# One weight unit loaded ahead of another expert's, a final gain row spread by TensorE, router products before two transposes

## The chip, the cores and the metric

The kernel runs on one core of a Trainium2 chip. The time is the device time of one execution in microseconds (us), and the times of the kernel before are a median of three runs. The engines are named as in the profile: PE is TensorE, DVE is VectorE, ACT is ScalarE, POOL is GpSimd and SP is SyncE. SPq and POOLq are the queues from which SP and POOL issue DMAs. PE is in order: what is written first is done first.

## The reference

A decoder trunk of two layers on 256 tokens of 1024 channels in float32. Each layer adds a mixer, a cross-attention into 256 memory tokens and a feed-forward part; the first layer's is dense, the second's picks two of eight experts for each token. A last norm follows.

```python
def moe_swiglu(xn, router_w, w13, w2):
    logits = (xt @ router_w).astype(jnp.float32)
    top_vals, top_idx = lax.top_k(logits, TOP_K)              # TOP_K = 2, N_EXPERTS = 8
    top_p = jax.nn.softmax(top_vals, axis=-1)
    ...
    for e in range(N_EXPERTS):
        out = out + gates[:, e:e + 1] * swiglu(xt, w13[e], w2[e])   # w13[e]: 1024 x 7168, w2[e]: 3584 x 1024
...
x = x + moe_swiglu(hn, router_w[layer // 2], w13_moe[layer // 2], w2_moe[layer // 2])
return rmsnorm(x, final_norm_g)
```

## The kernel before

**Experts as items.** The eight experts are eight "items". Item 0 and the even ones have room for 96 tokens ("mid", `mid_x`), item 1 and the odd ones for 64 ("few", `few_x`). The weights of an item are 42 units of 1 MiB (`ITEM_UNITS`), read in seven steps j = 0..6: four units of the up projection, then two of the down projection of the step before. So 336 units pass through the chip, each is loaded once and used once, in float32. The order in which PE reads them is the list `READS`: 12 units of item 0 (`HEAD`, two steps), the whole of item 1, the other 30 of item 0 (`BODY`), then items 2 to 7. Item 0's expert is fixed, so its units may be loaded before the router has decided; item 1's may not.

**Buffers and the order of loads.** There are 20 slots of 1 MiB (`RING`), and a twenty-first (`slot_once`, `pool_at`) that is used once. The list `LOADS` is the order in which SP issues the loads: 20 units of item 0 (`EARLY`), the 42 of item 1, the other 22 of item 0, then items 2 to 7. Below, load n is the entry n of that list, counted from 0. `rooms_of_loads()` gives each load after the twentieth the slot of a unit already read, and SP waits on `units_read` until PE has read it: load 20 waits for the first read, and from load 35 on load n waits for read n-19. One load, `EXTRA`, goes into `slot_once` and waits on `routed`, which DVE raises at the end of the routing. SP issues strictly in order. Between the 20 early loads and load 20 it waits on `info_ready` (L573) and reads two values (`info`: the number of items, item 1's expert).

**Steps of one item on PE.** In `item()`, PE calls `between(j)`, then transposes `hidden` (L2316), multiplies four up units (L2252) and two down units (L2252). ACT applies Silu (L987) and copies the transposed hidden values (L978); DVE multiplies (L1644). `between(j)` is where other work is put into an item: `lay_out`, `back`, `gather_pair`, and in the last item `lay_x` (L2214), four products of 128x512 that lay the residual stream into PSUM.

**Router.** The residual stream `x` is transposed on PE (`turn_plain` L1805, `turn_quarter` L2103) and `route()` (L2113) forms the logits from the transposed halves. The last quarter of `x` comes from DVE in two parts (`x_quarter`, `x_part`, L1387). ACT and DVE copy the transposes out (`lower_xT`, `quarter_xT`, `upper_xT`). From the logits DVE finds the two experts of each token, the places and the order of the items.

**Gains.** The weights of each norm are one row of 1024 values. `load_gain` on POOL (L614) reads the row 128 times over, 512 KB, into `g_row` on 128 partitions, as soon as the norm before has used the old one. The last norm's go this way too. DVE uses them first in item 7 (`weigh_x`) and ACT and DVE write the output after that.

## Time and profile before

| what | value |
|---|---|
| median of 3 runs (lowest, highest) | 1334.89 us (1334.65, 1335.25) |
| the profiled execution, its own time | 1334.52 us |
| its span, first to last instruction | 1332.7 us |
| granted clock of TensorE, mean | 0.998 |
| PE busy | 1310.0 us (98%) |
| DVE, ACT, POOL busy | 407.1, 333.3, 14.8 us |
| DMA moved | 444.27 MB |
| expert weights among it | 336 units of 1024 KB |

The page gives busy times of each engine and cuts the span into 40 equal slices (33.3 us each) with a digit for the share of each. The slices of the expert part begin with the sixteenth, at about 500 us. In them both PE and DMA show digits of 9, so the page alone does not say which of the two limits the expert part; that has to be read from the waits and from the time that a load takes from its issue to its landing. A matmul of float32 is two records in the trace (x8 are four), and successive records overlap, so a price is read from the distance of their starts.

### The profile page before, as it was taken

Reading aid. Unit: us, or ns where it says so; the run is one execution under the profiler, and the core shown is the slowest. Engines: PE = TensorE matmul, PEld = TensorE weight load, DVE = VectorE, ACT = ScalarE, POOL = GpSimd, SP = SyncE. Lnnn points to the kernel's source line nnn. Section 1 sums busy time; section 2 is a strip of 40 time slices with the busy share of each in tenths; the row PEclk is TensorE's granted clock in tenths of the full one; section 3 lists DMA queues with packets and bytes.
Section 4 is the critical chain, followed back from the end, with each engine's and each line's share of the span. In section 5 each row is a group of like instructions: output and inputs, shape, how many; then the busy total and the mean of one; then the engine's idle time right before and its main releaser. Section 6 shows DMA issues by size and latency. Waiting matters only on the chain.

```text
span 1332.7 us, 24929 instructions
## 1 busy us (share of the span) xinstructions
PE 1310.0 (98%) x10817; PEld 857.7 (64%) x10817; DVE 407.1 (31%) x778; ACT 333.3 (25%) x629; POOL 14.8 (1%) x28
## 2 busy tenths in 40 slices
PE   9999999999999999998999999999999999999987
PEld 6989888888798986432667666335666335666322
DVE  6686754444748765000111100101100101100201
ACT  6565554443646642000001000001000001000002
POOL 1100000000000000000000000000000000000000
PEclk9999999999999999999999999999999999999999
DMA  8935255554543689999999999999999999999995
GB/s 322 336 130 225 95 188 186 187 187 187 185 178 120 250 341 368 405 423 421 420 420 420 420 408 396 413 420 420 420 420 419 420 421 420 419 421 419 421 421 241
DMA packets 63913, 444.27 MB, mean 333 GB/s; under 512 B 7293, under 2 KB 8717, under 8 KB 10936
## 3 DMA queue, kind: packets, MB, share of 16 engines
q1 hardware_dynamic: 61976, 437.22, 81.4%
q0 software_dynamic: 1824, 5.42, 1.1%
q8 instruction: 87, 1.43, 0.4%
q14 instruction: 26, 0.21, 0.0%
HBM read 441.17 MB, written 1.44 MB: 332 GB/s over the span
## 4 chain that ended last, share of the span: by engine, by line
PE 91%; DMA 4%; SPq 2%; DVE 2%; ACT 1%; issue 1%; DVEq 0%; ACTq 0%
PE up_banks L2252 34%; PE bank L2252 16%; PE bank L1752 7%; PE bank L1754 7%; PE bank L1753 7%; DMA raw<-in_moe_units 4%; PE up_banks L1752 3%; PE up_banks L1754 3%; PE up_banks L1753 3%; SPq L536 2%; PE bank L2316 1%; PE bank L2199 1%; PE bank L1847 1%; PE bank L2229 1%; PE bank L1794 1%; DVE w_lo L1053 1%
## 5 line engine op out<-in xcount | busy, mean ns | idle before, releaser
L1644 DVE TENSOR_TENSOR hidden<-hidden,up_banks 128x384 f32<-128x384 f32 (+1 forms) x56 | 27.3, 487 | 582.7 <-ACT hidden L987 582.7
L1053 DVE TENSOR_TENSOR w_lo<-raw,w_hi 128x1024 fp32r<-128x1024 f32 x154 | 181.5, 1219 | 42.0 <-ACT w_hi L660 40.7
L660 ACT ACTIVATE w_hi<-raw 128x1024 fp32r<-128x1024 f32 x154 | 155.2, 1057 | 47.6 <-PE bank L1754 39.6
L987 ACT ACTIVATE hidden<-up_banks 128x384 f32<-128x384 f32 (+1 forms) x56 | 24.5, 437 | 475.3 <-PE up_banks L2252 475.3
L2252 PE MATMUL up_banks<-raw,mid_x 128*32 128x256 f32 (+1 forms) x1260 | 95.0, 450 | 0.0
L2252 PE MATMUL bank<-raw,hT 128*32 128x256 f32 (+2 forms) x716 | 82.1, 486 | 2.7 <-DMA raw<-in_moe_units 2.6
L1752 PE MATMUL bank<-xT_hi,w_hi 128*128 128x256 f32 x288 | 82.5, 287 | 0.0
L1753 PE MATMUL bank<-xT_lo,w_hi 128*128 128x256 f32 x288 | 81.5, 283 | 0.0
L1754 PE MATMUL bank<-xT_hi,w_lo 128*128 128x256 f32 x288 | 81.4, 283 | 0.0
L2252 PEld LDWEIGHTS up_banks<-raw,mid_x 128*32 128x32 f32 x1260 | 57.4, 110 | 33.3 <-issue 1.6
L978 ACT ACTIVATE hT<-bank 128x384 f32<-128x384 f32 (+1 forms) x56 | 24.5, 437 | 209.2 <-PE bank L2316 209.2
L2252 PE MATMUL up_banks<-raw,few_x 128*64 128x512 f32 x296 | 67.7, 595 | 0.5 <-DMA raw<-in_moe_units 0.5
L2252 PEld LDWEIGHTS bank<-raw,hT 128*32 128x32 f32 (+1 forms) x716 | 38.7, 116 | 41.2 <-issue 25.1
L1752 PEld LDWEIGHTS bank<-xT_hi,w_hi 128*128 128x128 f32 x288 | 55.2, 192 | 1.4 <-issue 1.3
L1753 PEld LDWEIGHTS bank<-xT_lo,w_hi 128*128 128x128 f32 x288 | 55.2, 192 | 0.1
L1754 PEld LDWEIGHTS bank<-xT_hi,w_lo 128*128 128x128 f32 x288 | 55.2, 192 | 0.0
L1752 PE MATMUL bank<-w_hi,yT_hi 128*128 128x512 f32 x136 | 53.7, 395 | 0.4 <-DVE w_lo L1053 0.3
L1754 PE MATMUL bank<-w_hi,yT_lo 128*128 128x512 f32 x136 | 53.0, 390 | 0.0
L1753 PE MATMUL bank<-w_lo,yT_hi 128*128 128x512 f32 x136 | 52.9, 389 | 0.0
L2252 PE MATMUL up_banks<-slot_w_hi,mid_x 128*32 128x256 f32 (+1 forms) x648 | 50.3, 451 | 0.0
L2252 PE MATMUL up_banks<-slot_w_lo,mid_x 128*32 128x256 f32 (+1 forms) x612 | 47.5, 450 | 0.0
L2252 PEld LDWEIGHTS up_banks<-raw,few_x 128*64 128x64 f32 x296 | 20.6, 137 | 40.5 <-issue 39.1
(421 smaller groups left out, 2099.7 us busy)
## 6 DMA issues: line engine op xcount, KB each, us to landing
raw<-in_moe_units SPq DMA_DIRECT2D x109, 1024.0 KB, 23.0
slot_w_hi<-in_moe_units SPq DMA_DIRECT2D x46, 1024.0 KB, 23.8
slot_w_lo<-in_moe_units SPq DMA_DIRECT2D x46, 1024.0 KB, 24.2
raw<-in_layer_units SPq DMA_DIRECT2D x44, 1024.0 KB, 4.9
raw<-in_dense_units SPq DMA_DIRECT2D x33, 1024.0 KB, 4.8
slot_bias<-in_moe_units SPq DMA_DIRECT2D x19, 1024.0 KB, 22.7
slot_xT_lo<-in_moe_units SPq DMA_DIRECT2D x18, 1024.0 KB, 22.9
slot_xT_hi<-in_moe_units SPq DMA_DIRECT2D x18, 1024.0 KB, 22.8
```

Source lines behind the costliest of these rows:

```text
L536: sp.dma_start(slots[slot], src).then_inc(sem(f"in{slot}"), 16)
L660: act.activation(w_hi[:, st.split(u), half, :], raw[:, st.slot(u), half * n:(half + 1) * n], ACT.Copy)\
L978: act.activation(hT[:, j % 2, 0:n, :], bank[3][:, 0:n * P].rearrange("p (b r) -> p b r", b=n), ACT.Copy)\
L987: act.activation(hidden_of(n), ups_of(n, 1), ACT.Silu).then_inc(sem("silu"), 1)
L1053: dve.tensor_tensor(w_lo[:, st.split(u), half, :], raw[:, st.slot(u), half * n:(half + 1) * n], w_hi[:, st.split(u), half, :].bitcast(F32) ...
L1644: dve.tensor_tensor(hidden_of(n), hidden_of(n), ups_of(n, 0), ALU.mult)\
L1752: pe.matmul(out, hi_l, hi_r, start=start, stop=False, skip_group_check=True)
L1753: pe.matmul(out, hi_l, lo_r, start=False, stop=False, skip_group_check=True)
L1754: return pe.matmul(out, lo_l, hi_r, start=False, stop=stop, skip_group_check=True)
L1794: mm = pe.transpose(bank[b][:, k * P:(k + 1) * P], xn[:, t, a:a + P], ident)
L1847: pe.matmul(bank[6][:, :], conv_u[:, 0, 0:P], conv_u[:, :, 0:T], start=True, stop=True)
L2252: return pe.matmul(out, rows, moving, start=start, stop=stop, skip_group_check=True)
```

## The change

Three things are changed.

1. `AHEAD = RING + 1`: one more unit of item 0 (the twenty-first of `HEAD + BODY`) is loaded before item 1's units, and SP issues it before it waits on `info_ready`. It waits for the first read. `EXTRA`, the load into `slot_once`, becomes item 1's unit 1 in place of its unit 2, so that it is still load 22. Every unit of item 1 is one place later in `LOADS`; from load 63 on the order is as before.
2. The last norm's gains are loaded as one row of 4 KB (POOL, same wait) and spread to 128 partitions by two PE products of 128x512 (`spread_gain`) with a row of ones, in item 2 ahead of step 5; ACT copies them out in two (`gain_rows`), before that step's Silu. DVE waits for those copies (`last_gain`) in item 7 in place of the DMA.
3. `route(0, 0)`, four products, stands before the two `turn_quarter`s instead of between them.

```diff
--- before.py
+++ after.py
@@ -60,6 +60,7 @@
 HEAD = (*range(10), 14, 15)
 BODY = tuple(u for u in range(ITEM_UNITS) if u not in HEAD)
 EARLY = (HEAD + BODY)[:RING]
+AHEAD = RING + 1
 
 
 SKEW_W, SKEW_P = 384, 32
@@ -239,11 +240,11 @@
 
 LATER = [unit for i in range(2, NE) for unit in whole(i)]
 READS = of_first(HEAD) + whole(1) + of_first(BODY) + LATER
-LOADS = of_first(EARLY) + whole(1) + of_first((HEAD + BODY)[RING:]) + LATER
+LOADS = of_first((HEAD + BODY)[:AHEAD]) + whole(1) + of_first((HEAD + BODY)[AHEAD:]) + LATER
 
 
 READ_NO = {unit: n + 1 for n, unit in enumerate(READS)}
-EXTRA = (1, 2)
+EXTRA = (1, 1)
 
 
 def rooms_of_loads():
@@ -489,6 +490,7 @@
     last_banks = (6, 7, 1, 5)
     weighed_bank = 0
     pair_banks = (2, 6, 7)
+    gain_banks = (2, 6)
     xlogit_banks = (2, 3, 6, 7)
 
     def heads_of_pair(b, t):
@@ -569,6 +571,13 @@
         for n in range(1, RING):
             hold(sp, *room[n])
             load_unit(item_units(0), EARLY[n], moe[EARLY[n]])
+
+        def load_first(units):
+            for u in units:
+                hold(sp, "units_read", item_units(0).room(u))
+                load_unit(item_units(0), u, moe[u])
+
+        load_first((HEAD + BODY)[RING:AHEAD])
         sp.wait_ge(sem("info_ready"), 1)
         n_items = sp.value_load(info[0:1, 0:1], min_val=NE, max_val=ITEMS)
 
@@ -582,9 +591,7 @@
                 load_unit(item_units(i), u, moe[e * ITEM_UNITS + u])
 
         load_item(1)
-        for u in (HEAD + BODY)[RING:]:
-            hold(sp, "units_read", item_units(0).room(u))
-            load_unit(item_units(0), u, moe[u])
+        load_first((HEAD + BODY)[AHEAD:])
         for i in range(2, NE):
             load_item(i)
         with sp.If(n_items > NE):
@@ -643,7 +650,10 @@
                 pool.dma_start(less8[:, :, :], io["less8"]).then_inc(sem("router_in"), 16)
                 pool.dma_start(row_ids[:, :], io["row_ids"]).then_inc(sem("router_in"), 16)
             load_gain(l * 3 + 3, io["ffn_norm_g"][l])
-            load_gain(l * 3 + 4, io["mix_norm_g"][l + 1] if l + 1 < DEPTH else io["final_norm_g"])
+            if l + 1 < DEPTH:
+                load_gain(l * 3 + 4, io["mix_norm_g"][l + 1])
+        pool.wait_ge(sem("xn_ready"), (3 * DEPTH + 1) * 4)
+        pool.dma_start(g_row[0:1, :], io["final_norm_g"].rearrange("(o d) -> o d", o=1)).then_inc(sem("gain_in"), 16)
 
 
     @block.scalar
@@ -970,6 +980,12 @@
                 last = act.activation(to[:, 512:768], bank[5][:, 0:256], ACT.Copy)
             last.then_inc(sem("y_hi"), 1)
 
+        def gain_rows():
+
+            act.wait_ge(sem("gain_mm"), 1)
+            for half, b in enumerate(gain_banks):
+                act.activation(g_row[:, half * 512:(half + 1) * 512], bank[b][:, :], ACT.Copy).then_inc(sem("last_gain"), 1)
+
         def item(i, units, many, begin=0, end=ITEM_STEPS, first_in=None):
             n = 3 if many else 2
 
@@ -983,6 +999,8 @@
                     if j == 1 and first_in is not None:
                         first_in()
                     turned_hidden(j - 1)
+                if j == 5 and isinstance(i, int) and i == 2:
+                    gain_rows()
                 act.wait_ge(sem("units_read"), units.read(3 if j == 0 else 6 * j + 1))
                 act.activation(hidden_of(n), ups_of(n, 1), ACT.Silu).then_inc(sem("silu"), 1)
             turned_hidden(end - 1)
@@ -1689,7 +1707,7 @@
                                              iota[:, 0:FEW].unsqueeze(1).broadcast_to([P, 2, FEW]), 1.0,
                                              pos[:, t, i:i + 1], ALU.add, ALU.is_equal)
                 last.then_inc(sem("select"), 1)
-                dve.wait_ge(sem("gain_in"), 16 * (3 * DEPTH + 1))
+                dve.wait_ge(sem("last_gain"), 2)
                 dve.wait_ge(sem("added"), i * 4)
                 weigh_x()
             gated(i, 3, many)
@@ -2115,9 +2133,9 @@
             if upper:
                 mm.then_inc(sem("router_mm"), 1)
 
+        route(0, 0)
         pe.wait_ge(sem("x_quarter"), 1)
         turn_quarter(4, 7).then_inc(sem("quarter_mm"), 1)
-        route(0, 0)
         pe.wait_ge(sem("x_part"), 4 * (3 * DEPTH - 2) + 4)
         turn_quarter(6, 1).then_inc(sem("xT_mm"), 1)
         route(0, 1)
@@ -2218,6 +2236,13 @@
 
             pe.wait_ge(sem("weighed_x"), times)
             pe.matmul(bank[weighed_bank][:, :], ident, weighed_x[:, :], start=True, stop=False, skip_group_check=True)
+
+        def spread_gain():
+
+            pe.wait_ge(sem("gain_in"), 16 * (3 * DEPTH + 1))
+            for half, b in enumerate(gain_banks):
+                mm = pe.matmul(bank[b][:, :], mats[0:1, 2, :], g_row[0:1, half * 512:(half + 1) * 512], start=True, stop=True)
+            mm.then_inc(sem("gain_mm"), 1)
 
         def lay_out(i):
 
@@ -2389,6 +2414,8 @@
                 elif j == 3:
                     pe.wait_ge(sem("added"), i * 4)
                     lay_out(i)
+                elif j == 5 and i == 2:
+                    spread_gain()
                 elif j == 4 and i == NE - 1:
                     weigh_rows(i)
                 elif j == 6 and i == NE - 1:
```

On SP, at the end of the early loads. Before (the names are the slots; `slot_bias_49` is the slot of the very first unit):

```order
L536 DMA slot_yT_lo_62<-in_moe_units 128x2048 [waits unit_used]
L573 TENSOR_LOAD info [waits info_ready]
L573 ISA x2
L576 TENSOR_LOAD info
L576 ISA x2
L536 ISA [waits units_read]
L536 DMA slot_bias_49<-in_moe_units 128x2048
L536 ISA [waits units_read]
L536 DMA raw<-in_moe_units 128x2048
L536 ISA [waits routed]
L536 DMA slot_once<-in_moe_units 128x2048
```

After the change:

```order
L538 DMA slot_yT_lo_62<-in_moe_units 128x2048 [waits unit_used]
L538 DMA slot_bias_49<-in_moe_units 128x2048 [waits units_read]
L582 TENSOR_LOAD info [waits info_ready]
L582 ISA x2
L585 TENSOR_LOAD info
L585 ISA x2
L538 ISA [waits units_read]
L538 DMA raw<-in_moe_units 128x2048
L538 ISA [waits routed]
L538 DMA slot_once<-in_moe_units 128x2048
L538 ISA [waits units_read]
L538 DMA raw<-in_moe_units 128x2048
```

The load into `slot_bias_49` has moved from behind the wait on `info_ready` and the two value loads to ahead of them.

On PE, the end of the last projection and the router products (`mats,x` are transposes of x, `plain_xT,pool_inv` the router products). Before:

```order
L1805 MATMUL bank<-mats,x 128x128 [waits x_part,router_gain]
L1805 MATMUL bank<-mats,x 128x128 x3
L2103 MATMUL bank<-mats,x 128x128 [waits x_quarter]
L2103 MATMUL bank<-mats,x 128x128
L2113 MATMUL up_banks<-plain_xT,pool_inv 32x128 [waits lower_xT]
L2113 MATMUL up_banks<-plain_xT,pool_inv 32x128 x3
L2103 MATMUL up_banks<-mats,x 128x128 [waits x_part]
L2103 MATMUL up_banks<-mats,x 128x128
L2113 MATMUL up_banks<-plain_xT,pool_inv 32x128 [waits upper_xT]
L2113 MATMUL up_banks<-plain_xT,pool_inv 32x128 x3
L2113 MATMUL bank<-plain_xT,pool_inv 32x128 [waits lower_xT]
```

After the change:

```order
L1823 MATMUL bank<-mats,x 128x128 [waits x_part,router_gain]
L1823 MATMUL bank<-mats,x 128x128 x3
L2131 MATMUL up_banks<-plain_xT,pool_inv 32x128 [waits lower_xT]
L2131 MATMUL up_banks<-plain_xT,pool_inv 32x128 x3
L2121 MATMUL bank<-mats,x 128x128 [waits x_quarter]
L2121 MATMUL bank<-mats,x 128x128
L2121 MATMUL up_banks<-mats,x 128x128 [waits x_part]
L2121 MATMUL up_banks<-mats,x 128x128
L2131 MATMUL up_banks<-plain_xT,pool_inv 32x128 [waits upper_xT]
L2131 MATMUL up_banks<-plain_xT,pool_inv 32x128 x3
L2131 MATMUL bank<-plain_xT,pool_inv 32x128 [waits lower_xT]
```

The router products with `lower_xT` have moved above both transposes, so the second transpose follows the first directly.

On PE in item 2, between the second down unit of step 3 and step 5's first up unit. Before:

```order
L2252 MATMUL bank<-raw,hT 32x512 [waits in2]
L2252 MATMUL bank<-raw,hT 32x512 x2
L2252 MATMUL bank<-raw,hT 32x256 x6
L2252 MATMUL bank<-raw,hT 32x512 x3
L2252 MATMUL bank<-raw,hT 32x256 x6
L2316 MATMUL bank<-mats,hidden 128x128 [waits hid_ready]
L2316 MATMUL bank<-mats,hidden 128x128 x2
L2252 MATMUL up_banks<-raw,mid_x 32x512 [waits in3]
L2252 MATMUL up_banks<-raw,mid_x 32x512 x2
L2252 MATMUL up_banks<-raw,mid_x 32x256 x6
L2252 MATMUL up_banks<-raw,mid_x 32x512 x3
```

After the change:

```order
L2277 MATMUL bank<-slot_xT_hi_51,hT 32x512 x2
L2277 MATMUL bank<-slot_xT_hi_51,hT 32x256 x6
L2277 MATMUL bank<-slot_xT_hi_51,hT 32x512 x3
L2277 MATMUL bank<-slot_xT_hi_51,hT 32x256 x6
L2244 MATMUL bank<-g_row,mats 128x512 [waits gain_in]
L2244 MATMUL bank<-g_row,mats 128x512
L2341 MATMUL bank<-mats,hidden 128x128 [waits hid_ready]
L2341 MATMUL bank<-mats,hidden 128x128 x2
L2277 MATMUL up_banks<-slot_w_hi_52,mid_x 32x512 [waits in7]
L2277 MATMUL up_banks<-slot_w_hi_52,mid_x 32x512 x2
L2277 MATMUL up_banks<-slot_w_hi_52,mid_x 32x256 x6
```

Two rows of 128x512 with `g_row` stand ahead of the transposes of `hidden` that were there before.

## Rows read from the trace of the kernel before

**Rows 1.** The page: its span, its GB/s by 40 slices, one DMA issue line.
```profile
span 1332.7 us, 24929 instructions
...
GB/s 322 336 130 225 95 188 186 187 187 187 185 178 120 250 341 368 405 423 421 420 420 420 420 408 396 413 420 420 420 420 419 420 421 420 419 421 419 421 421 241
...
g_row<-in_final_norm_g POOLq DMA_DIRECT2D x1, 512.0 KB, 9.9
```

**Rows 2.** Windows: stretch and length, busy PE PEld DVE ACT POOL, PEclk, DMA, GB/s.
```profile
515.00:520.00 5.00, 5.00 (x76) 3.13 (x72) 4.55 (x23) 0.61 (x1) 0.00 (x0) 1.00 0.71 282
520.00:525.00 5.00, 5.00 (x61) 2.78 (x54) 0.53 (x2) 0.49 (x1) 0.00 (x0) 1.00 0.89 356
...
631.00:718.00 87.00, 86.95 (x1134) 57.18 (x1136) 8.92 (x20) 7.27 (x17) 0.00 (x0) 1.00 1.01 420
718.00:770.00 52.00, 52.00 (x694) 34.99 (x690) 7.55 (x15) 3.81 (x8) 0.00 (x0) 1.00 1.01 420
770.00:840.00 70.00, 70.00 (x903) 43.30 (x896) 3.24 (x6) 4.79 (x10) 0.00 (x0) 1.00 1.00 398
```

**Rows 3.** Chain of waits, end of item 1 and end of the span: start, length, what.
```profile
603.74 25.30 DMA raw<-in_moe_units
...
1293.99 26.35 DMA raw<-in_moe_units
1320.39 1.96 PE bank L2252 x8
```

**Rows 4.** Timeline of SP's issues: start, length, what.
```profile
518.04 0.36 SPq L536 DMA_DIRECT2D slot_bias<-in_moe_units  x1
518.99 0.34 SPq L536 DMA_DIRECT2D raw<-in_moe_units  x1
...
534.40 0.33 SPq L536 DMA_DIRECT2D slot_xT_hi<-in_moe_units  x1
```

**Rows 5.** Timeline of PE in item 0's head: the units' first records.
```profile
515.95 7.96 PE L2252 MATMUL up_banks<-raw,mid_x 128*32 128x512 f32 x108
...
531.37 2.79 PE L2252 MATMUL up_banks<-slot_xT_hi,mid_x 128*32 128x512 f32 x36
533.95 2.80 PE L2252 MATMUL up_banks<-slot_w_hi,mid_x 128*32 128x512 f32 x36
```

**Rows 6.** Line L536, 457:469: four lone loads, issue to landing.
```profile
L536 SPq DMA_DIRECT2D raw<-in_moe_units x4: 327/328/328, 457.9 to 468.0; - x4
...
DMA to landing us min/median/max: 4.6/4.9/5.0
```

**Rows 7.** The same of load 20 alone, issued at 518.04.
```profile
L536 SPq DMA_DIRECT2D slot_bias<-in_moe_units x1: 360/360/360, 518.0 to 518.0; - x1
...
DMA to landing us min/median/max: 5.1/5.1/5.1
```

**Rows 8.** The same of load 32 alone, issued at 548.40.
```profile
L536 SPq DMA_DIRECT2D slot_memT_lo<-in_moe_units x1: 333/333/333, 548.4 to 548.4; - x1
...
DMA to landing us min/median/max: 6.6/6.6/6.6
```

**Rows 9.** The same of load 145 alone, late in item 2.
```profile
L536 SPq DMA_DIRECT2D slot_w_lo<-in_moe_units x1: 333/333/333, 834.9 to 834.9; - x1
...
DMA to landing us min/median/max: 6.9/6.9/6.9
```

**Rows 10.** Timeline of PE at the router: last transposes and the router products.
```profile
502.71 0.60 PE L1805 MATMUL bank<-mats,x 128*128 128x128 f32 x4
503.39 0.44 PE L2103 MATMUL bank<-mats,x 128*128 128x128 f32 x2
503.76 0.43 PE L2113 MATMUL up_banks<-plain_xT,pool_inv 128*32 128x128 f32 x8
504.11 0.44 PE L2103 MATMUL up_banks<-mats,x 128*128 128x128 f32 x2
504.48 0.43 PE L2113 MATMUL up_banks<-plain_xT,pool_inv 128*32 128x128 f32 x8
```

**Rows 11.** Timeline of PE in item 7: products of 128x512 in float32 (`lay_x`).
```profile
1304.28 1.02 PE L2214 MATMUL up_banks<-x,mats 128*128 128x512 f32 x2
1305.14 1.02 PE L2214 MATMUL bank<-x,mats 128*128 128x512 f32 x2
1305.99 0.38 PE L2316 MATMUL bank<-mats,hidden 128*128 128x128 f32 x2
```

## The prediction

> **What bounds the kernel now.** The page's GB/s line comes first [rows 1]: from the expert part on it stands at about 420, whatever PE does. 1024 KB at 420 GB/s is 2.49 us for one unit. The chain of waits says where that matters. Item 1 ends with a load issued at 603.74 that lands 25.30 us later, and the span ends with one issued at 1293.99 that lands 26.35 us later, after which PE has only its last unit left [rows 3]. With lone loads landing in 4.6 to 5.0 us [rows 6], the other 20 us of each are queue: the DMA stream is the limit, and the end moves with the place of the last load in it. From the last landing to the end nothing is changed that takes time.
>
> Two places can move that stream. The first is its gap. In 515:520 the DMA share is 0.71 and in 520:525 it is 0.89 [rows 2], some 2.0 us without data, because load 20 is issued only at 518.04 [rows 4]. The second is where the queue is nearly empty, since there a later issue costs time at once. In a mid item PE takes 2.58 us for a unit (starts at 531.37 and 533.95 [rows 5]), plus its turns, against the stream's 2.49, so through items 0 and 2 PE loses ground and the slots come free later and later. The loads' times to landing tell how much is left: 6.6 us for load 32 [rows 8] and 6.9 us for load 145 at 834.9 [rows 9]. If a lone load takes 4.9 us, the median of [rows 6], load 32 has 1.7 us of queue before it and load 145 has 2.0 us. After that item 3, a few item, refills the queue. Between 631 and 840 PE is busy 208.95 of 209 us [rows 2], so what is added to PE there is added to every read behind it.
>
> **Router products ahead of the turns.** PE's second quarter turn starts at 504.11, and between it and the first stand four products (eight records) that start at 503.76 [rows 10]. In front of both turns they fall partly into the gap between the last half's transposes, about 0.44 us of issue from 502.71, and the first turn at 503.39. The first turn then starts some 0.12 us later; the second, on which the last copies and products hang, starts at about 503.88 in place of 504.11. I take 0.23 us, between nothing (if a copy of ACT ends last) and 0.36, the distance of such a group's starts. All of the routing, PE's first expert unit and all later issues by reads move by it.
>
> **One more load ahead.** An issue follows PE's next unit by 0.45 us: the unit at 533.95 [rows 5] and the issue at 534.40 [rows 4]. The first read is marked by the unit at 515.95 [rows 5], so the new load 20 goes out at 516.40, less 0.23, 516.17, in place of 518.04. It is alone, so it lands after 4.9 to 5.1 us [rows 6, 7]. Load 21 is set by the second read already (518.99 [rows 4], 518.76 with the 0.23) and lands at 523.7, against 518.04 + 5.1 + 2.49 = 525.6 before. So the stream gains 1.9 to 2.0 us there. Later issues follow reads as before, and at load 32 the gain can be no more than its queue and the 0.23: 1.7 + 0.23 = 1.9 us. Both bounds agree; I take 1.9. If lone loads take 4.6 us it is 2.0, with 5.1 it is 1.7.
>
> This is not yet the end. Item 1's units have moved one place back, and PE reads its last one as it lands [rows 3]. That landing shifts by 2.49 - 1.9 = +0.6 us. PE begins the rest of item 0 0.6 us later, and has no idle time in which to make it good.
>
> **The gain row.** The DMA of 512 KB becomes 4 KB. At 420 GB/s that is 1.2 us of transfer; it was issued at about 506.5 and took 9.9 us to land [rows 1], so all of it lies ahead of the gap. The early loads land 1.2 us sooner, PE doesn't read them yet, and the gap only starts sooner: worth nothing. In exchange PE gets two products of 128x512. The nearest rows are those of item 7, whose starts stand 0.86 us apart (1304.28, 1305.14, and the next work at 1305.99) [rows 11]: 1.72 us, all added since PE is never idle there. The bounds are 0.9 us, if the single row makes them cheaper, and 2.0 us with a bubble at the change of shape. ACT's two copies lie in its wait for the up products, on its own queue ahead of one Silu whose units last 10 us; they cost nothing. DVE's new wait, in item 7, was met long before. SP has one issue moved, none added.
>
> **The sum.** In item 2 PE is late by 0.6 + 1.72 = 2.3 us, and load 145's issue with it. It has 2.0 us of queue before it, and what isn't covered shifts its landing: +0.3 us. From there the stream runs without a gap to the end, so the end moves by +0.3 us, and the 1.9 us gained at 518 are gone: between the two places PE's reads, not the stream, hand on the time. With L for a lone load, the shift is 2.49 - (6.6 - L + 0.23) + 1.72 - (6.9 - L) = 2L - 9.5 us: -0.3 for 4.6, +0.3 for 4.9, +0.7 for 5.1. The profiled execution took 1334.52 us, its span 1332.7; the sum gives 1334.8. The median of the runs stands 0.37 us above it, so I predict 1334.89 + 0.3 = **1335.2 us**.
>
> The Trainium skill, page "DMA: Bandwidth & Descriptors", section "Anatomy of one DMA", fits a DMA as 2.0 us plus bytes over 436 GB/s. That is 4.4 us for a unit, and an estimate by it gives -0.7 us. Its fit is for POOL's path; rows 6 have 4.6 to 5.0 and decide.
>
> **Rivals.**
>
> *The stream keeps its gain.* If PE's lateness never reaches an empty queue, the end moves by the 1.9 us gained in the gap: 1333.0 us. That takes no more than 0.1 us of lateness in item 2 at L = 4.9, or units that take longer than PE's 2.58, so that the queue grows in mid items too. The GB/s of 398 in 770:840 against 420 [rows 2] speaks a little for it: the stream itself is slow there. Against it speaks 6.9 us at load 145, the end of a queue that has been shrinking. Chance 0.15. The same page's "Specifications" gives a limit of about 358 GB/s per core, by which a unit would take 2.93 us and this rival would hold; rows 2 with 420 say otherwise, and the chance stands as it was.
>
> *The load ahead is not early.* If it lands no sooner than the old load 20 did, because PE's first read comes about when the values are read, only the 0.23 is left of the gain: 2.49 - 0.23 + 1.72 - 2.0 = +2.0 us, 1336.9 us. It decides by the issue of load 20: at 516.2 it is wrong, near 518 right. The read at 515.95 speaks against it. Chance 0.10. This one is slower than before, as is the next.
>
> *A load behind another needs more than a lone one.* The term 2L takes both queues as usable down to the last 4.9 us. If a load with one other in flight can't land in under 6.1 us, the shift is 2 x 6.1 - 9.5 = +2.7 us, and from there on the change is slower by over 0.2%; at 6.5 us it is +3.5 us, 1338.4 us. The trace shows 6.6 as the least in the expert stream outside the gap, which leaves it open; load 20's 5.1 is against it. Chance 0.07.
>
> **How the numbers follow.** The forecast, with L from 4.6 to 5.1 and the products from 0.9 to 2.0 us, gets 0.65; 0.03 is left for what I don't see. Its own range is 1334.0 to 1336.0. The range of 8 in 10 takes in the first two rivals: **1333.0 to 1336.9 us**. What a measurement of this kernel can tell from no change is 0.2%, 2.7 us. Slower by more than that is the third rival, 0.07; faster by more than that needs over 2.7 us where the gap has 2.0, 0.03; within it 0.90.
>
> **What would show it.** Load 20 issued near 516.2 and landing in about 5 us. Item 1's last unit landing 0.6 us later than at 629.0. PE's two products 1.7 us together in item 2. Load 145 issued about 2.3 us later and landing in about 4.9 us instead of 6.9: that is the step that decides. If it still takes 6 us or more, the sum is wrong in PE's terms; if load 32 does not fall towards 4.9, it is wrong in the gap's. The last landing would be at about 1320.6. If the pauses that the stream makes by itself (398 GB/s) come elsewhere, all of this shifts by some tenths.

## The result: 4.2 us slower, and the profile after

The changed kernel takes 1339.05 us, median of 9 runs (1337.23 to 1340.22), against 1334.89 us for 9 runs of the kernel before (1332.9 to 1336.28). The ratio is 1.0032, interval [1.0024, 1.0040]: slower by 3.2 to 5.3 us. The forecast was 1335.2 us and its range ended at 1336.9.

The profiled execution of the changed kernel took 1340.22 us, the slowest of its nine runs, so its trace may hold something that a median run doesn't. The page of after, to be read beside [rows 1] (span, GB/s in 40 slices):

```profile
span 1338.4 us, 24939 instructions
...
GB/s 319 344 131 214 102 195 186 188 187 189 184 157 147 247 332 378 391 422 422 420 420 420 409 406 355 408 421 421 420 419 420 421 421 420 419 420 419 421 421 226
```

In the expert part the difference is in the slices (33 us each) just behind the gap (17th: 391 instead of 405 GB/s) and in those of item 2 (23rd to 26th: 409, 406, 355, 408 instead of 420, 408, 396, 413). From the 27th on both kernels move 420 GB/s. The chain of waits (start, length, what) says the same at its two landings, the end of item 1 and the end of the span:

```profile
605.71 25.13 DMA slot_w_lo<-in_moe_units
...
630.89 1.94 PE bank L2277 x8
...
1298.69 26.36 DMA raw<-in_moe_units
...
1325.09 1.96 PE bank L2277 x8
```

Item 1's last unit lands at 605.71 + 25.13 = 630.84, and before at 603.74 + 25.30 = 629.04 [rows 3]: it is 1.8 us later. PE begins the last unit of all at 1325.09 instead of 1320.39 [rows 3], 4.7 us later. The work of PE, ACT and DVE behind that is as long as before (DVE's last instruction starts at 1333.55 instead of 1328.85, 4.7 us later too). The output's DMA behind it ends 1.0 us later still; from the last landing to the end the traces take 12.4 to 13.7 us, whatever the kernel, and the kernel before has the least of it. So the traces are compared below by this landing and not by their spans.

**The head** (the first units of item 0, around the gap at 518). SP's issues (timeline: start, length, what), to be read beside [rows 4]:

```profile
515.64 0.33 SPq L538 DMA_DIRECT2D slot_bias<-in_moe_units  x1
518.38 0.36 SPq L538 DMA_DIRECT2D raw<-in_moe_units  x1
519.66 0.34 SPq L538 DMA_DIRECT2D slot_once<-in_moe_units  x1
```

Load 20 is issued at 515.64 (forecast 516.17, before 518.04) and lands 5.0 us later, as forecast. Yet the windows (columns as in [rows 2]) show that the stream does not stay full behind it:

```profile
515.00:520.00 5.00, 5.00 (x76) 3.14 (x72) 3.98 (x19) 0.00 (x0) 0.00 (x0) 1.00 0.74 275
520.00:525.00 5.00, 5.00 (x57) 2.40 (x49) 0.95 (x3) 0.49 (x1) 0.00 (x0) 1.00 0.91 321
...
770.00:840.00 70.00, 70.00 (x912) 43.76 (x904) 2.22 (x4) 4.91 (x10) 0.00 (x0) 0.98 0.95 380
```

The rest of the gap only moves: 275 GB/s instead of 282 in the first 5 us, 321 instead of 356 in the next. By the trace's landings load 20 is in 2.6 us earlier than before and load 21 2.3 us earlier, but load 33 only 0.2 us. In 770:840, where load 145 stands, the stream moves 380 GB/s instead of 398 [rows 2].

**Load 145.** The line of SP's loads, at the issue of load 145 (first line: durations in ns and start), and what it took to land:

```profile
L538 SPq DMA_DIRECT2D slot_memT_lo<-in_moe_units x1: 333/333/333, 840.3 to 840.3; - x1
...
DMA to landing us min/median/max: 7.0/7.0/7.0
```

It is issued 5.4 us later than before (840.3 against 834.9 [rows 9]) and still takes 7.0 us where it took 6.9. The forecast had it fall to 4.9. So at load 145 nothing of PE's 5.4 us of lateness is absorbed in this execution. Yet loads a little before it did come down to the time of a lone one, those issued at 808.0 (load 133) and at 824.1 to 829.3 (loads 139 to 141), each while the load before it was still in flight:

```profile
L538 SPq DMA_DIRECT2D slot_w_lo<-in_moe_units x1: 333/333/333, 808.0 to 808.0; - x1
...
DMA to landing us min/median/max: 4.9/4.9/4.9
...
DMA to landing us min/median/max: 5.1/5.2/5.3
```

Loads 142 and 145 then land 3.8 and 4.0 us after the one before instead of 2.49, and that brings load 145 back to 7.0. So the queue was used up, and the stream lost time on top of that.

**PE in item 2** (timeline: start, length, what):

```profile
795.52 2.82 PE L2277 MATMUL bank<-slot_xT_hi,hT 128*32 128x512 f32 x36
798.27 1.98 PE L2244 MATMUL bank<-g_row,mats 1*128 1x512 f32 x4
800.18 0.55 PE L2341 MATMUL bank<-mats,hidden 128*128 128x128 f32 x3
800.66 4.49 PE L2277 MATMUL up_banks<-slot_w_hi,mid_x 128*32 128x512 f32 x36
804.95 2.78 PE L2277 MATMUL up_banks<-slot_w_lo,mid_x 128*32 128x512 f32 x36
```

The two products of `spread_gain` (line 2244) hold PE from 798.27 to the start of the next work at 800.18: 1.9 us, forecast 1.72. The unit behind them takes 4.49 us where its neighbours take 2.8, and the granted clock says why (windows, the same columns, PEclk third from the end):

```profile
802.00:803.00 1.00, 1.00 (x12) 0.45 (x8) 0.00 (x0) 0.23 (x1) 0.00 (x0) 0.50 0.99 418
803.00:804.00 1.00, 1.00 (x10) 0.54 (x6) 0.00 (x0) 0.00 (x0) 0.00 (x0) 0.50 0.58 229
804.00:805.00 1.00, 1.00 (x17) 0.52 (x13) 0.00 (x0) 0.00 (x0) 0.00 (x0) 0.60 0.12 49
805.00:806.00 1.00, 1.00 (x18) 0.59 (x14) 0.00 (x0) 0.00 (x0) 0.00 (x0) 1.00 0.00 0
```

For some 3.4 us TensorE ran at half clock (0.5, which is 1.2 of 2.4 GHz), though PE was never idle ahead of it. That costs 1.7 us, and the DMA share falls to 0 behind it: the queue was empty. The Trainium skill, page "TensorE: Matmul & The Clock Gate", section "What's actually happening", has these two levels and ties the lower one to an engine that was not busy. The trace doesn't agree: here PE had been busy without a break, with two products whose operands hold 1 of 128 rows just ahead.

So there were two candidates for the 4.2 us. **Theory A**: the clock. The products of one row make it fall, and that is most of the loss. **Theory Q**: the queue, which is the prediction's third rival. A load behind others needs more time than a lone one, so neither the gain in the gap nor load 145's 2.0 us is really there, and each microsecond of PE goes to the end. The expectations of the first four runs name a **theory B** in its place, that the unit moved ahead of item 1 is what costs; **theory L**, in later ones, is the forecast's, by which the queue can be used down to 4.9 us.

### The profile page after: what moved, and what is told of

Read it like the earlier page. It is cut to its first block, busy times and chain, and to the rows that moved or that the text cites. A ratio compares the mean times of both kernels' runs of the same rounds, so it can differ in the third digit from the quotient of the medians.

```text
span 1338.4 us, 24939 instructions
## 1 busy us (share of the span) xinstructions
PE 1313.6 (98%) x10821; PEld 858.4 (64%) x10821; DVE 407.1 (30%) x778; ACT 334.8 (25%) x631; POOL 14.8 (1%) x28
## 4 chain that ended last, share of the span: by engine, by line
PE 77%; SPq 14%; DMA 5%; DVE 2%; issue 1%; ACT 1%; DVEq 0%; ACTq 0%
PE up_banks L2277 26%; SPq L538 14%; PE bank L2277 12%; PE bank L1770 7%; PE bank L1772 7%; PE bank L1771 7%; DMA slot_w_lo<-in_moe_units 3%; PE up_banks L1770 3%; PE up_banks L1772 3%; PE up_banks L1771 3%; DMA raw<-in_moe_units 2%; PE bank L2341 1%; PE bank L1865 1%; PE bank L1812 1%; PE bank L2217 1%
```

## The experiments

Each was timed in 5 rounds beside the kernel before, whose medians in the three groups that ran together were 1335.08, 1334.73 and 1334.68 us. Ratios are to it, with their 95% interval, and a time in brackets behind one is ratio minus 1 times 1335; its interval reaches some 1.2 us to either side. "PE at 145" is the shift against before, in the profiled execution, of the unit on which load 145's issue waits, and "last landing" that of the last load.

### The load ahead alone

```diff
+AHEAD = RING + 1
-LOADS = of_first(EARLY) + whole(1) + of_first((HEAD + BODY)[RING:]) + LATER
+LOADS = of_first((HEAD + BODY)[:AHEAD]) + whole(1) + of_first((HEAD + BODY)[AHEAD:]) + LATER
-EXTRA = (1, 2)
+EXTRA = (1, 1)
...
+        load_first((HEAD + BODY)[RING:AHEAD])
         sp.wait_ge(sem("info_ready"), 1)
```

> Before with part 1 alone (one more load of item 0 ahead, EXTRA moved). Theory A, PE's clock: the loss comes mainly from the one-row products, so here PE is late by 1.2 to 1.8 us at the end of item 1 (2.49 us less what the stream gains in its gap) and nothing is added in item 2; load 145's queue of 2 us covers it, and the end moves by -0.5 to +0.5 us. Theory B, the order of loads: the unit moved ahead of item 1 is what costs, and the end moves by +2 to +4 us. Load 20 should be issued at about 516.4 and no clock fall should appear in item 2 under either.

Measured: 1337.18 us, 1.0019 [1.0010, 1.0029] (+2.5 us). Its gap is closed better than in the changed kernel's trace, and the gain is lost all the same (windows):

```profile
515.00:520.00 5.00, 5.00 (x76) 3.11 (x68) 3.94 (x19) 0.00 (x0) 0.00 (x0) 1.00 1.01 393
520.00:525.00 5.00, 5.00 (x57) 2.40 (x48) 0.95 (x3) 0.49 (x1) 0.00 (x0) 1.00 0.99 398
530.00:555.00 25.00, 24.51 (x271) 13.16 (x260) 0.58 (x2) 1.91 (x4) 0.00 (x0) 1.00 0.96 371
```

In 530:555, some ten loads behind the gap, it moves 371 GB/s; the kernel before moved there:

```profile
530.00:555.00 25.00, 25.00 (x281) 13.58 (x270) 0.55 (x1) 1.52 (x3) 0.00 (x0) 1.00 1.01 408
```

37 GB/s for 25 us is 0.9 MB, 2.2 us of stream. Load 33 lands only 0.3 us earlier than before, item 1's last landing comes 2.4 us later, nearly the whole 2.49 us of the place, and both PE at 145 (+2.4) and the last landing (+2.5) follow. This part alone makes more than half of the loss: theory A's -0.5 to +0.5 us did not come, with no half clock at work.

### The gain row alone

```diff
+        pool.dma_start(g_row[0:1, :], io["final_norm_g"].rearrange("(o d) -> o d", o=1)).then_inc(sem("gain_in"), 16)
...
+                mm = pe.matmul(bank[b][:, :], mats[0:1, 2, :], g_row[0:1, half * 512:(half + 1) * 512], start=True, stop=True)
...
+                elif j == 5 and i == 2:
+                    spread_gain()
```

> Before with part 2 alone (gain row of 4 KB, two one-row products in item 2). Theory A: the granted clock falls to about 0.5 for 3 to 4 us right after the products, PE is late by 3.4 to 3.8 us from there on, load 145's queue of 2.0 us covers a part, and the end moves by +1.2 to +2.0 us. Theory B: the products cost 1.8 us, which the queue covers, and the end moves by 0 to +0.3 us.

Measured: 1337.00 us, 1.0012 [1.0003, 1.0021] (+1.6 us). PE at 145 is 1.95 us later, the two products, and the clock did not fall in its trace. The time lies in the range that was expected of theory A, but PE was not late by the 3.4 to 3.8 us that should have made it, so the number is no support for A. With the load ahead (+2.5) this makes 4.1 us, about the changed kernel's +4.2: within the intervals the parts add up, and no half clock is needed in the sum.

### Full rows in place of one row

On the changed kernel; it loads the 512 KB again and multiplies 128 rows by the identity.

```diff
-                mm = pe.matmul(bank[b][:, :], mats[0:1, 2, :], g_row[0:1, half * 512:(half + 1) * 512], start=True, stop=True)
+                mm = pe.matmul(bank[b][:, :], ident, g_row[:, half * 512:(half + 1) * 512], start=True, stop=True)
```

> The changed kernel, but the gains are loaded on all 128 partitions as before and the two products take all 128 rows of them against the identity matrix; same place, same size, same copies. Theory A (few rows at work let the clock fall): the clock stays at 1.00 in item 2, PE is late by 1.8 us less than in the changed kernel (3.6 in place of 5.4 us), and the end is 1.5 to 1.8 us earlier than the changed kernel's, some +2.9 us against before. If any change of shape of the products were enough for the clock, it falls here too and the end stays at +4 to +4.5 us.

Measured: 1339.70 us, 1.0033 [1.0020, 1.0045] (+4.4 us). There is no half clock in its trace, and it is no faster than the changed kernel. What A expected did not come. Nor did the 512 KB, which it loads again, cost anything that these medians can show.

### The products in item 1

On the changed kernel; they stand in step 5 of item 1, where PE waits for the stream.

```diff
+            elif j == 5:
+                pe.wait_ge(sem("spread"), 1)
+                spread_gain()
...
-                elif j == 5 and i == 2:
-                    spread_gain()
```

> The changed kernel with the two one-row products and their copies in item 1 ahead of step 5, where PE waits for loads anyway. Theory A: the clock may fall there too, but PE has about 0.8 us of idle time per unit there, so that item 1 still ends with its last landing; nothing is added in item 2 and the end moves by -0.5 to +0.8 us against before, that is 3.5 to 4.5 us less than the changed kernel. Theory B: the end stays at +2 to +4 us.

Measured: 1337.24 us, 1.0014 [1.0005, 1.0023] (+1.9 us). PE at 145 is +1.9 us, as it already is at the end of item 1: the products have vanished in PE's wait there. It is as fast as the load ahead alone. So what the products cost depends on their place.

### Two full products more, and four, in item 2

On the kernel before; their results are not used. The lines of the second have `range(4)`.

```diff
+        def more_products():
+
+            for n in range(2):
+                pe.matmul(bank[(2, 6)[n % 2]][:, :], ident, x[:, 0, 0:512], start=True, stop=True, skip_group_check=True)
...
+                elif j == 5 and i == 2:
+                    more_products()
```

> Before with two more full products of 128x512 on PE in item 2 ahead of step 5, into banks that nothing reads; nothing else is changed. PE is late by 1.72 us from there. Theory Q (a thin queue slows the stream long before it is empty; only latencies above about 7 us are free): hardly any of the lateness is covered at load 145 with its 6.9 us, and the end moves by +1.2 to +1.8 us. Theory L of the forecast (the queue can be used down to 4.9 us): the 2.0 us of queue cover it and the end moves by 0 to +0.3 us.

Measured: 1336.71 us, 1.0015 [1.0006, 1.0024] (+2.0 us).

> Before with four more full products of 128x512 on PE in item 2 ahead of step 5 (two in e5_two_more). PE is late by 3.4 us. Theory Q: nothing of it is covered beyond some tenths, the end moves by +3.0 to +3.6 us. Theory L: 2.0 us are covered, +1.4 us.

Measured: 1338.50 us, 1.0033 [1.0022, 1.0043] (+4.4 us). These two are nothing but PE time, at full rows, with no change to any load. The chain of waits of the one with two products, the end of item 1 and the end of the span:

```profile
603.47 25.31 DMA raw<-in_moe_units
...
628.82 1.94 PE bank L2257 x8
...
1296.04 26.31 DMA raw<-in_moe_units
...
1322.39 1.96 PE bank L2257 x8
```

Item 1's last unit lands 0.3 us earlier than before, and the last unit begins 2.0 us later [rows 3], with PE 1.5 us later at load 145. That load is issued at 836.4 and takes 8.1 us. By the prediction its 2.0 us of queue would have swallowed those 1.5.

### PE made earlier in item 2

On the kernel before. Four (the first) or two (the second) of item 2's accumulated blocks are left out, so that PE is 5.2 or 2.6 us faster there.

```diff
+                        if isinstance(i, int) and i == 2 and j in (2, 3) and k in (1, 3):
+                            continue
```

> Before with four of item 2's 56 row-block products of the up projection left out (channel blocks 1 and 3 in steps 2 and 3), so part of the expert's sum is missing; PE is 5.2 us earlier from about 770 on, the loads are the same. Theory Q: the queue at load 145 is deep enough to keep the pace, the extra pauses of loads 119 to 146 (3.8 us in the trace of before) largely go, and the end moves by -1 to -2.5 us. Rival (the pauses belong to the memory and come in any case, the stream is the limit throughout): the end does not move, within 0.3 us.

Measured: 1332.85 us, 0.9983 [0.9974, 0.9992] (-2.3 us).

> Before with two of the blocks of item 2 left out (channel blocks 1 and 3 of step 2, half of e10_item2_lighter), so part of that expert's sum is missing; PE is 2.6 us earlier. Theory Q: load 145 takes about 8.5 us, the stream keeps most of its pace, the end moves by -1.0 to -1.9 us, nearly all that e10 gave. If the rate rises only with a much deeper queue, it is half of e10's, -0.8 to -1.0 us.

Measured: 1333.26 us, 0.9992 [0.9983, 1.0001] (-1.1 us, which alone can't be told from none). The windows of 770:840, first with 5.2 us less:

```profile
770.00:840.00 70.00, 70.00 (x853) 41.95 (x845) 5.21 (x11) 5.08 (x11) 0.00 (x0) 1.00 1.01 420
```

and with 2.6 us less:

```profile
770.00:840.00 70.00, 70.00 (x875) 42.98 (x866) 4.66 (x9) 5.30 (x12) 0.00 (x0) 1.00 1.01 413
```

So the 398 GB/s of the kernel before [rows 2] were not a habit of the stream: with loads issued earlier it moves 420. In the lighter one load 145 took:

```profile
L536 SPq DMA_DIRECT2D slot_w_lo<-in_moe_units x1: 332/332/332, 828.9 to 828.9; - x1
...
DMA to landing us min/median/max: 11.8/11.8/11.8
```

In their traces PE is 3.6 us early at load 145 with two blocks less and 6.0 us with four, but the last landing only 2.4 and 1.7 us. The medians stand the other way round (-1.1 and -2.3 us), with intervals that overlap; both views say that earlier issues bring some 1 to 2.5 us and no more, though PE is early by up to 6. The kernel before thus already lost about 2 us in item 2 to a queue that was too short, at a load time of 6.9 us.

### The load ahead, with a lighter head

The load ahead alone, with two blocks of item 0's step 1 left out: PE is 2.6 us faster there.

```diff
+                        if isinstance(i, int) and i == 0 and begin == 0 and j == 1 and k in (1, 3):
+                            continue
```

> Part 1 alone (as in e1_ahead_only), with two of the products' blocks of item 0's step 1 left out, so part of that expert's sum is missing; the reads from the fifth on come up to 2.6 us sooner, and so the issues of loads 25 to 34. Theory Q: in e1 the gain of the gap was lost at loads 22 to 34 because the queue there was thin (6.5 to 7 us); here load 33 lands 1.5 to 2.5 us earlier than before, item 1's last read is late by +0.3 to +1.0 us in place of +2.4, and the end moves by 0 to +0.8 us against before in place of +2.5. Rival (the gain was lost to pauses of the memory's own): load 33 about -0.3 us, item 1 +2.4 us, as in e1.

Measured: 1334.38 us, 0.9995 [0.9986, 1.0004] (-0.7 us, within what can be told from none). Its window:

```profile
530.00:555.00 25.00, 24.06 (x254) 12.45 (x247) 0.98 (x2) 2.29 (x5) 0.00 (x0) 1.00 1.01 421
```

421 GB/s instead of 371. Load 21 lands 1.8 us earlier than before and load 33 still 1.6 us, and item 1's last unit 1.0 us earlier, where it was expected 0.3 us or more later. With its loads issued earlier the stream doesn't give the gain back in these ten loads, as it does with the load ahead alone. The kernel before with the same lighter head was not run, so how much of the 1.6 us at load 33 would be there without the load ahead is not shown.

### The changed kernel again

> The changed kernel once more, on this chip and beside these runs. If the fall of the granted clock behind the one-row products comes only in some executions, this profile may show none; then PE is late by 3.6 us in place of 5.4 us from step 5 of item 2 on and the time stays at +3.3 to +4.3 us against before. If the clock falls each time, it is there again at about 801 and lasts 3.4 us.

Measured: 1339.06 us, 1.0031 [1.0020, 1.0042] (+4.1 us), the same as the first time. In this profiled execution the clock stayed up (PE's timeline):

```profile
798.73 1.98 PE L2244 MATMUL bank<-g_row,mats 1*128 1x512 f32 x4
800.64 0.55 PE L2341 MATMUL bank<-mats,hidden 128*128 128x128 f32 x3
801.12 2.80 PE L2277 MATMUL up_banks<-slot_w_hi,mid_x 128*32 128x512 f32 x36
```

The unit behind the products takes 2.80 us, not 4.49, PE at 145 is +4.2 us instead of +5.4, and the last landing +3.9 instead of +4.7. So the half clock is an event of some executions, and is not the 4.2 us.

The mean granted clock that each run lists says how often. Half clock for 3.4 us takes 0.0013 off the mean over 1338 us. The mean is 0.998 or 0.999 in all 80 runs of the edited kernels that have no products of one row and in the 87 of the kernel before beside them. It is 0.997 in 12 of the 49 runs of the four kernels that have them: 5 of 16 of the changed kernel, 4 of 11 of the gain row alone, 3 of 11 of the last kernel below, 0 of 11 with the products in item 1 (a reading of 0.998 can hide a fall). So the fall belongs to the products of one row. The changed kernel's 5 runs at 0.997 have a mean of 1339.8 us, its 11 others 1338.7, which is still 3.8 us above the kernel before. The clock costs some 1.1 us where it falls, and theory A's main claim, that it is most of the loss, is wrong.

### The load ahead with the router products, and the rest without the load ahead

The changed kernel without part 2, and the kernel before with part 3 and the gain row in item 1, but without the load ahead.

```diff
+        route(0, 0)
         pe.wait_ge(sem("x_quarter"), 1)
         turn_quarter(4, 7).then_inc(sem("quarter_mm"), 1)
-        route(0, 0)
```

> The changed kernel without its part 2: one more load ahead and the router products ahead of the turns, the gains loaded as before. Theory Q: like part 1 alone, less the 0.2 to 0.3 us of the router: the end at +1.7 to +2.3 us against before, item 1's last read at +1.8 to +2.4 us, no lateness added in item 2.

Measured: 1337.10 us, 1.0019 [1.0010, 1.0028] (+2.5 us), no less than the load ahead alone, though in its trace item 1's last unit comes 1.3 us later than before and not 2.4. The router's 0.24 us is too little for these medians to show.

> Before with the router products ahead of the turns and the gain row of 4 KB, its two products in item 1 ahead of step 5, where PE waits for loads; no load is moved ahead. Theory Q: PE is not late in items 0 and 2, the 1.8 us of the products lie in its waits of item 1, and the end moves by -0.5 to 0.0 us. If the products or the clock cost something there, it is +0.5 us or more.

Measured: 1334.77 us, 1.0002 [0.9993, 1.0011] (+0.3 us). Without the load ahead and with the products under item 1's wait the change costs nothing, and brings nothing that can be told. No version here that computes the whole result beats the kernel before.

## Why the prediction was wrong, step by step

**One table shows it.** The shifts against the kernel before, in the profiled executions. "Pauses" is worked out from the landings: the sum, over loads 119 to 146, of what each lands later than 2.48 us after the one before it.

| kernel | PE at 145 | last landing | GB/s in 770:840 | pauses |
|---|---|---|---|---|
| item 2 lighter by 5.2 | -6.0 | -1.7 | 420 | 1.6 |
| item 2 lighter by 2.6 | -3.6 | -2.4 | 413 | 1.2 |
| router, gain row in item 1 | -1.6 | -1.9 | 404 | 1.9 |
| load ahead, lighter head | -1.0 | -1.5 | 396 | 4.1 |
| before | 0 | 0 | 398 | 3.7 |
| load ahead and router | +1.3 | +1.9 | 392 | 5.6 |
| two products more | +1.5 | +2.0 | 394 | 5.5 |
| changed, products in item 1 | +1.9 | +2.1 | 394 | 5.0 |
| gain row alone | +2.0 | +3.0 | 392 | 5.9 |
| load ahead alone | +2.4 | +2.5 | 392 | 5.8 |
| changed, full rows | +3.6 | +3.8 | 391 | 6.3 |
| changed, again | +4.2 | +3.9 | 387 | 7.3 |
| four products more | +4.3 | +3.5 | 387 | 5.6 |
| changed, with the half clock | +5.4 | +4.7 | 380 | 8.4 |

From about -2 us upward the end follows PE nearly one for one, whatever made PE late or early: a load, products of one row or of 128, or work left out. Below that it stops following. The prediction had put that bend at +2.0. The edits that change nothing but PE's work in item 2 (two lighter, two heavier) move the pauses too, so these don't come by themselves: the later the loads are issued, the more the stream pauses. Single executions scatter by one to two microseconds (the kernel before: 1332.9 to 1336.28), which the column of the last landing shows too.

**What the stream does.** From the issue and landing times of loads 22 to 335 in the fourteen traces one can work out how much longer than 2.48 us after the load before it each load lands, sorted by how long after its own issue the load before it lands. Where that is over 10 us, the mean excess is 0.02 to 0.05 us; from 5 us on it is at most 0.09; from 4 to 5 us (192 loads) it is 0.18, and from 2 to 4 us (103 loads) 0.48 us. These are single pauses and not a slower pace: over 0.2 us late are 5% of the loads with more than 5 us, 26% of those with 4 to 5 and 56% of those with 2 to 4, by 0.7 to 0.8 us each on the mean, and the others keep their 2.48. A load issued when the one before has 4 us left to land would be in time if 4.9 us of a lone load were all it needed, since its turn comes 2.48 us later, at 6.5. Most are, but one in four isn't: the loss begins once a load's own time to landing comes under some 7.5 us. So theory Q holds in its consequence, that PE's lateness goes to the end long before the queue is empty, and not in its strict form: a load behind others can land as soon as a lone one, but the stream pauses more often there.

**Now the steps.**

- *Router products, 0.23 us*: right. The second turn's products start at 503.55 and the last transposes at 502.39, 1.16 us apart; [rows 10] have 504.11 and 502.71, 1.40. That is 0.24 us.
- *Load 20 issued at 516.17, landing in about 5 us*: right (515.64 and 5.0), and with it the rival "the load ahead is not early" falls.
- *The stream gains 1.9 us there, kept at load 32*: the first step that failed. The gain is there at load 21 (2.3 us), and 0.2 us of it is left at load 33. Load 32 was to fall from 6.6 towards 4.9 us and took 7.0, 6.9 with the load ahead alone. The stream made pauses, 3.2 us of them in loads 22 to 33 instead of 1.1, and 4.9 us instead of 3.3 in all from load 22 to item 1's last. The term "6.6 - L" with L = 4.9 was sized at 1.7 us; by item 1's last landing (2.49 us less its shift and less the router's 0.23) it is worth 0 to 0.4 us in the two traces of the changed kernel, and 0 to 1.0 us over the six traces that have the load ahead and a full head.
- *Item 1's last landing +0.6 us*: +1.8 measured, +2.3 in the second trace of the changed kernel, +2.4 with the load ahead alone. It follows from the step before.
- *Two products, 1.72 us*: right in kind and nearly in size: between item 1's end and load 145 PE loses 1.9 us with the products of one row (gain row alone; changed kernel again) and 1.8 us with full rows. ACT's copies, the 512 KB and DVE's wait: nothing, as said.
- *Load 145 has 2.0 us of queue*: the second step that failed, and the costlier one. Issued 5.4 us later it took 7.0 us, not 4.9; at +2.4 us 7.4, at +1.5 us 8.1. With the full rows (+3.6), four products more (+4.3) and the changed kernel again (+4.2) it did fall, to 5.7, 6.3 and 6.5 us, and the last landing came 3.5 to 3.9 us later all the same. The 2.0 us are there, but on the way to them the stream pauses for about as long as they are worth. The prediction called this the step that decides.

The sum by the measured terms: item 1's end is late by 1.8 to 2.3 us (the two traces of the changed kernel) and the products cost 1.9, together 3.7 to 4.2 us, against a median of +4.2. In the prediction's own formula, 2L - 9.5, it takes L = 6.6 to 6.9 to give that. Such an L says how much was lost; it is no time below which a load can't land, since loads 133 and 139 to 141 landed in 4.9 to 5.3 us with one or two others in flight. What the sum left out is a term for the pauses. The third rival had the direction and very nearly the time (1338.4 us), and had 0.07. Its mechanism, that a load with one other in flight can't land in under 6.1 us, is not what happened: these four loads refute it, and the time was met partly by luck. Right in it is that a queue close to empty is not free. The ground on which it was made small, that load 20 landed in 5.1 us, was weak: one load, issued with only the last 1.4 us of the load before it left. Load 21, issued 0.95 us behind it, took 7.6 us and landed 3.4 us after it, where the prediction counted 2.49. The evidence in the trace that spoke for a loss was read past: 6.6 us was the least time to landing in a stretch of hundreds of loads, and the 398 GB/s of 770:840 were already the price of the thin queue, since they became 420 with loads issued earlier. The prediction took them for the stream's own slowness and for a small support of its first rival. Its L also stood on thin rows: of the four loads of [rows 6] the second was issued 2.3 us behind the first, and in the changed kernel's trace the same four took 5.8 to 7.5 us. Two slips in its numbers change nothing here: its formula gives 1333.8 to 1335.9 us for the forecast's own range, not 1334.0 to 1336.0, and the chances inside the range called 8 in 10 add up to 0.90.

The Trainium skill, page "DMA: Bandwidth & Descriptors", section "Anatomy of one DMA", gives a DMA issued by POOL as a fixed 2.0 us and its bytes over the rate. That sizes one load by itself. The pauses above are what it leaves out: they become frequent with two to three loads in flight, the new one among them, and no run here measured the same with smaller loads.

**Still open.** Why the clock falls behind the products of one row in some executions only (it did in one of two traces of the changed kernel, and not in those of the gain row alone or of the products in item 1, which have the same two products); and why the stream pauses more often with two or three loads in flight than with more.

## What to carry to other kernels

When a stream of large loads runs beside an engine that frees its slots, don't count its queue down to a lone load's latency: take the least time to landing that the busy stretch itself shows as nearly empty, and read a GB/s a few per cent under the peak as loss that has begun. There, each microsecond of the other engine was about a microsecond of the end, so extra products belong where that engine waits (here in item 1, at no cost), and a load moved ahead of others can cost its whole 2.49 us at the place it pushed back, where the loads behind it are not issued earlier too (2.4 us with the load ahead alone).

## What the runs showed of the hardware

- The DMA stream of 1 MB loads moved 420 GB/s when a load took 12 us to land in item 2 (420 in 770:840), 398 when it took 7 (before), and 380 to 394 when PE was later still. Single loads kept the pace with 4.9 to 5.3 us to landing, but with so thin a queue more than half of them landed over 0.2 us behind it.
- A float32 product of 128x512 costs PE about as much when its operands hold 1 row (1.91 us for two, changed kernel) as with 128 rows (1.83 for two in its place).
- TensorE's granted clock fell to 0.5 for 3.4 us with PE busy throughout, right behind two products of one row, in one execution and not in another of the same kernel. It added 1.7 us to a unit of 2.8. Over all runs a mean clock of 0.997 came only in kernels with such products, in 12 of 49.
